# Eight of the 32 pieces of a transposed key cache are prepared during the attention instead of during and right after the input projection

## The reference, cut to what matters

```
h = rms_norm(x, g_pre_mix);  z = h @ w_in           # 2560 columns: q, k, v, a, gate
kc = concatenate([cache_win_k, k], axis=1)          # sample group: cached keys, then new ones
for window, dil in ((128, 1), (512, 4), (2048, 16)):
    idx = wb + t - dil * arange(129)
    s = einsum("bthd,btjhd->bthj", q, kc[:, idx]) * 64 ** -0.5
    o, lse = softmax(s) @ vc[:, idx], log of the denominator
attn = mixture of the three by their denominators
u = a * sigmoid(gate); c = silu(layer_norm(causal_dwconv(u, width 31)))
x = x + rms_norm(concat(rms_norm(attn), rms_norm(c)) @ w_out)
# then cross-attention into 256 memory rows, and a gated convolutional FFN
```

## Time and profile before

| | |
|---|---|
| median of three runs | 1789.27 us |
| the profiled execution's own time | 1791.59 us |
| its span | 1789.8 us |
| mean granted TensorE clock | 0.98 |
| PE busy | 94% |
| DVE busy | 62% |
| ACT busy | 52% |

### The profile page before, as it was taken

How to read it: one execution, slowest core, us unless ns; L and a number is a source line. 1 busy time by engine, 2 the same in 40 slices (tenths; PEclk the granted TensorE clock), 3 DMA queues, 4 the chain that set the end, 5 groups by cost and what they waited for, 6 DMA issues and landing times.

```text
span 1789.8 us, 29564 instructions
## 1 busy us (share of the span) xinstructions
PE 1689.1 (94%) x11614; PEld 1576.5 (88%) x11614; DVE 1110.3 (62%) x2050; ACT 927.0 (52%) x1680; POOL 2.2 (0%) x12
## 2 busy tenths in 40 slices
PE   7999889946999999999999889999999999999998
PEld 6999888924567999988778889999999999999998
DVE  5489896835775687444567567654576533676533
ACT  7444435653566776555456555444545533545533
POOL 0000000000000000000000000000000000000000
PEclk9999999968999999999999899999999999999999
DMA  9998979669432545543443334444444544444443
GB/s 314 242 247 198 231 178 211 130 202 332 170 114 87 170 147 166 163 131 120 144 131 115 94 114 134 141 130 141 132 141 150 151 132 143 130 141 145 146 135 105
DMA packets 417824, 284.02 MB, mean 159 GB/s; under 512 B 69675, under 2 KB 392353, under 8 KB 415887
## 3 DMA queue, kind: packets, MB, share of 16 engines
q1 hardware_dynamic: 412840, 273.31, 54.1%
q10 hardware_dynamic: 4847, 8.83, 1.5%
HBM read 226.97 MB, written 32.48 MB: 145 GB/s over the span
## 4 chain that ended last, share of the span: by engine, by line
PE 76%; DVE 6%; SPq 6%; ACT 5%; DMA 4%; issue 3%; DVEq 0%; ACTq 0%
PE bank L1341 71%; PE bank L1338 4%; DMA PLANES<-HALVES 2%; SPq L473 2%; SPq L528 1%; ACT whi L702 1%; SPq L518 1%; SPq L519 1%; DMA raw<-in_w_in_dram 1%; ACT WORDS L825 1%; DVE C L1931 1%; DVE cv L1931 1%; DVE wlo L1944 1%; DMA raw<-in_w_mk_dram 0%; DMA cached_t<-keys_turned 0%
## 5 line engine op out<-in xcount | busy, mean ns | idle before, releaser
L1944 DVE TENSOR_TENSOR wlo<-raw,whi 128x1024 fp32r<-128x1024 f32 (+1 forms) x312 | 374.3, 1201 | 274.3 <-ACT whi L702 274.0
L1341 PE MATMUL bank<-op_hi,whi 128*128 128x352 f32 x1632 | 539.3, 330 | 4.7 <-DVE wlo L1944 2.4
L1341 PE MATMUL bank<-op_hi,wlo 128*128 128x352 f32 x1632 | 525.8, 322 | 0.0
L1341 PE MATMUL bank<-op_lo,whi 128*128 128x352 f32 x1632 | 524.6, 321 | 0.0
L702 ACT ACTIVATE whi<-raw 128x1024 fp32r<-128x1024 f32 (+1 forms) x312 | 325.1, 1043 | 330.0 <-DMA raw<-in_w_up_dram 92.3
L1341 PEld LDWEIGHTS bank<-op_hi,whi 128*128 128x128 f32 x1632 | 307.4, 188 | 14.3 <-issue 10.5
L1341 PEld LDWEIGHTS bank<-op_lo,whi 128*128 128x128 f32 x1632 | 308.4, 189 | 0.6
L1341 PEld LDWEIGHTS bank<-op_hi,wlo 128*128 128x128 f32 x1632 | 307.4, 188 | 0.0
L1341 PE MATMUL bank<-fhi,whi 128*128 128x352 f32 x528 | 171.1, 324 | 0.0
L1341 PE MATMUL bank<-fhi,wlo 128*128 128x352 f32 x528 | 170.8, 323 | 0.0
L1341 PE MATMUL bank<-h1hi,whi 128*128 128x352 f32 x480 | 160.8, 335 | 3.3 <-DVE wlo L1944 3.3
(11 more groups left out here) (284 smaller groups left out, 2229.7 us busy)
## 6 DMA issues: line engine op xcount, KB each, us to landing
raw<-in_w_up_dram SPq DMA_DIRECT2D x132, 512.0 KB, 3.8
raw<-in_w_down_dram SPq DMA_DIRECT2D x48, 512.0 KB, 4.1
PLANES<-HALVES SPq DMA_DIRECT2D x128, 112.0 KB, 3.7
keys_turned<-WORDS SPq DMA_DIRECT2D x32, 448.0 KB, 3.2
cached_t<-keys_turned SPq DMA_DIRECT2D x8, 1792.0 KB, 8.9
raw<-in_w_out_dram SPq DMA_DIRECT2D x24, 512.0 KB, 4.2
raw<-in_w_xq_dram SPq DMA_DIRECT2D x24, 512.0 KB, 4.1
raw<-in_w_xo_dram SPq DMA_DIRECT2D x24, 512.0 KB, 4.2
```

The costliest lines, as they stand in the source:

```text
L1341: return pe.matmul(out, lhsT, rhs, start=first, stop=last, skip_group_check=shared)
L1944: dve.tensor_tensor(wlo[v % SLOTS][:, 0:nk, :], raw[v % SLOTS][:, 0:nk, :], whi[v % SLOTS][:, 0:nk, :].bitcast(F32), ALU.subtract).then_in ...
```

## The change

Pieces 24 to 31 (sequences 6 and 7) are called LATE. The other 24 are spread over the projection, one to a call place at most, and end before its end. The late ones get their own buffers for halves, planes and words in the first three weight slots, which stand empty until the output projection, and a semaphore name of their own for the joins. SP calls the stream for two of them behind each of windows 3 to 7. ACT joins them at slots r = 10, 16, 18, 23, 25, 30, 32, 39 of the first group, ahead of whatever else that slot holds. The three weight loads of the output projection move from before the V outputs to behind window 7 and the last piece. Two of the three places for windows are swapped, so that window 1 no longer waits for the convolution and window 2 does; three small tiles (STD) move out of the way.

```diff
...
@@ -209,13 +209,15 @@
     stage_f = mn("stage_f", 146656, [P, 3, P])
 
 
-    PLACES = (47104, 119808, 160064)
+    PLACES = (47104, 160064, 119808)
     cached = [mn(f"cached{i}", o, [P, KTILES, AW]) for i, o in enumerate(PLACES)]
     cached_t = [mn(f"cached_t{i}", o, [P, AT, KEYS]) for i, o in enumerate(PLACES)]
     HALVES = [mn(f"HALVES{i}", 160064 + 3584 * i, [P, 2, KEYS], U16) for i in range(2)]
     PLANES = [mn(f"PLANES{i}", 160064 + 7168 + 3584 * i, [P, 2, KEYS], U16) for i in range(2)]
     WORDS = [place(f"WORDS{i}", TAB + 3584 * i, [P, KEYS]) for i in range(2)]
-    WORDS += [place("WORDS2", RING, [P, KEYS]), place("WORDS3", RING + 5504, [P, KEYS])]
+    HALVES += [place(f"HALVES{2 + i}", RING + 3584 * i, [P, 2, KEYS], U16) for i in range(2)]
+    PLANES += [place(f"PLANES{2 + i}", RING + 3584 * (2 + i), [P, 2, KEYS], U16) for i in range(2)]
+    WORDS += [place(f"WORDS{2 + i}", RING + 3584 * (4 + i), [P, KEYS]) for i in range(2)]
     ATT = mn("ATT", 20480, [P, AT, NTOK])
     Pp = [mn("Pp0", 0, [P, 2, SEQ]), mn("Pp1", 8192, [P, 2, SEQ]), place("Pp2", RING + 8192 * (SLOTS - 1), [P, 2, SEQ])]
     PT = mn("PT", 38912, [P, 2, SEQ])
@@ -240,7 +242,7 @@
     XT = [mn("XT0", 20480, [P, NT, CW]), mn("XT1", 31744, [P, NT, CW]), mn("XT2", 0, [P, NT, CW])]
     xtok = [mn(f"xtok{i}", o, [P, D]) for i, o in enumerate((11264, 15360, 43008, 160064, 164160, 168256))]
     Yb = [mn(f"Y{i}", o, [P, NT, CW]) for i, o in enumerate((50176, 129024, 140288))]
-    STD = [place(f"STD{i}", RING + 8192 * i + 4096, [P, CW]) for i in range(CH)]
+    STD = [place("STD0", RING + 21504, [P, CW]), place("STD1", RING + 22912, [P, CW]), mn("STD2", 37376, [P, CW])]
     SQ = [mn(f"SQ{i}", 129024 + 1408 * i, [P, CW]) for i in range(4)]
     CSUM = [mn(f"CSUM{i}", o, [P, CW]) for i, o in enumerate((125440, 126848, 122624))]
     SQA = [mn(f"SQA{i}", 134656 + 1408 * i, [P, CW]) for i in range(4)]
@@ -369,15 +371,17 @@
         return n, n % len(cached)
 
     PIECES = AT * BD
-    LATE = PIECES - 4
-    PIECES_AT = {u: 1 for u in (*range(NT, 3 * NT, 2), 9, 13, 15, 19, 23, *range(3 * NT, XFIRST))}
-    PIECES_AT.update({24: 2, 28: 2, 32: 2, XFIRST: 2, XFIRST + 1: 2})
+    LATE = PIECES - 8
+    PIECES_AT = {u: 1 for u in (*range(NT, 3 * NT, 2), 11, 15, 19, 23, *range(3 * NT, XFIRST), XFIRST)}
 
     def pieces_until(u):
         return sum(n for v, n in PIECES_AT.items() if v < u)
 
-    def words_of(p):
-        return WORDS[p % 2 + (2 if p >= LATE else 0)]
+    def place_of(p):
+        return p % 2 + (2 if p >= LATE else 0)
+
+    def joined_by(p):
+        return "joined_late" if p >= LATE else "joined"
 
     def batch_slot(r):
 
@@ -512,7 +516,7 @@
                 sp.wait_ge(*at(f"planes{p % 2}", (p - 2, 1, 1)))
             if k == 0:
                 sp.wait_ge(*at(f"gathered{b % 2}", b))
-            t, name = HALVES[p % 2], f"turned{p % 2}"
+            t, name = HALVES[place_of(p)], f"turned{p % 2}"
             cols = slice(2 * P * k, 2 * P * (k + 1))
             near = A["cache_win_k"][0, b].rearrange("s h d -> s (h d)").bitcast(U16)[WB - NEAR:WB, cols]
             sp.dma_start_transpose(t[:, :, OLD:KEYS], near).then_inc(*mark(name, (p, "near"), 16))
@@ -522,24 +526,24 @@
 
             sp.wait_ge(*at(f"turned{p % 2}", (p, "old")))
             if p >= 2:
-                sp.wait_ge(*at("joined", (p - 2, 1)))
+                sp.wait_ge(*at(joined_by(p - 2), (p - 2, 1)))
             for e in range(2):
                 for h in range(2):
-                    sp.dma_start(PLANES[p % 2][DH * e:DH * e + DH, h, :], HALVES[p % 2][h:P:2, e, :]).then_inc(*mark(f"planes{p % 2}", (p, e, h), 16))
+                    sp.dma_start(PLANES[place_of(p)][DH * e:DH * e + DH, h, :], HALVES[place_of(p)][h:P:2, e, :]).then_inc(*mark(f"planes{p % 2}", (p, e, h), 16))
 
         def keep_keys(p):
 
             b, k = divmod(p, AT)
-            sp.wait_ge(*at("joined", (p, 1)))
-            sp.dma_start(A["keys_turned"][b, :, k, :], words_of(p)[:, :]).then_inc(*mark(f"kept{p % 2}", p, 16))
-
-        def key_stream(p):
-
-            if p < PIECES:
+            sp.wait_ge(*at(joined_by(p), (p, 1)))
+            sp.dma_start(A["keys_turned"][b, :, k, :], WORDS[place_of(p)][:, :]).then_inc(*mark(f"kept{p % 2}", p, 16))
+
+        def key_stream(p, first, end):
+
+            if first <= p < end:
                 turn_keys(p)
-            if 0 <= p - 1 < PIECES:
+            if first <= p - 1 < end:
                 part_keys(p - 1)
-            if 0 <= p - 2 < PIECES:
+            if first <= p - 2 < end:
                 keep_keys(p - 2)
 
         load(ident[:, :], A["identity"], "ident")
@@ -556,7 +560,7 @@
             if SLOTS <= u < SLOTS + BD:
                 gather_old(u - SLOTS)
             for _ in range(PIECES_AT.get(u, 0)):
-                key_stream(p)
+                key_stream(p, 0, LATE)
                 p += 1
             if u == SLOTS + 1:
                 load(stage_p[0:KW * CT, 1, :], A["conv_w"].rearrange("a t (k p) -> (a t k) p", p=P), "states", "cw")
@@ -568,27 +572,18 @@
                 for i in range(2):
                     load(stage_u[:, i, :], A["state_conv"].rearrange("a b t c -> (a b t) c")[i * 120:(i + 1) * 120, :], "states", ("u", i))
 
-        while p < LATE + 2:
-            key_stream(p)
-            p += 1
+        for p in range(p, LATE + 2):
+            key_stream(p, 0, LATE)
         for i in range(2):
             sp.wait_ge(*at(f"kept{i}", LATE - 2 + i))
         load(wt[:, :], A["prompt_bias"], "tables", "p")
         load(ws[:, :], A["sample_bias"], "tables", "s")
-        key_stream(LATE + 2)
+        window(1)
         sp.wait_ge(*at("unit", LAST_IN))
         window(0)
-        for p in range(LATE + 3, PIECES + 2):
-            key_stream(p)
         sp.wait_ge(*at("csq_used", 2 * CH - 1))
         sp.wait_ge(*at("cn", (CONV_ORDER[CH - 1], CT - 1)))
-        window(1)
-        sp.wait_ge(*at("joined", (PIECES - 1, 1)))
         window(2)
-        for u in range(XFIRST, XFIRST + SLOTS - 1):
-            for i in range(2):
-                sp.wait_ge(*at(f"kept{i}", PIECES - 2 + i))
-            weight(u)
         sp.wait_ge(*at("ztok", ("v", AT - 1, 2)))
         for t in range(TT):
             sp.dma_start(O["win_v_p"][0, 0, t * P:(t + 1) * P].rearrange("s h d -> s (h d)"), V[:, t, :]).then_inc(*mark("v_out", t, 16))
@@ -605,6 +600,14 @@
             else:
                 sp.wait_ge(*at("spv", b))
             window(n)
+            if n < 8:
+                for p in range(LATE + 2 * (n - 3), LATE + 2 * (n - 2)):
+                    key_stream(p, LATE, PIECES)
+            if n == 7:
+                for u in range(XFIRST, XFIRST + SLOTS - 1):
+                    for i in range(2):
+                        sp.wait_ge(*at(f"kept{i}", PIECES - 2 + i))
+                    weight(u)
         for e in range(2):
             sp.wait_ge(*at("ptr", (LAST_P2, parts_of(STEPS[LAST_P2][0]) - 1, e)))
         weight(XFIRST + SLOTS - 1)
@@ -818,11 +822,9 @@
             act.wait_ge(*at(f"planes{p % 2}", (p, 1, 1)))
             if p >= 2:
                 act.wait_ge(*at(f"kept{p % 2}", p - 2))
-            if p in (LATE, LATE + 1):
-                act.wait_ge(*at("unit", LAST_IN - 3 + p % 2))
-            words = words_of(p)[:, :].bitcast(U16).rearrange("p (n h) -> p h n", h=2)
+            words = WORDS[place_of(p)][:, :].bitcast(U16).rearrange("p (n h) -> p h n", h=2)
             for h in range(2):
-                act.activation(words[:, h, :], PLANES[p % 2][:, h, :], ACT.Copy).then_inc(*mark("joined", (p, h)))
+                act.activation(words[:, h, :], PLANES[place_of(p)][:, h, :], ACT.Copy).then_inc(*mark(joined_by(p), (p, h)))
 
         def join_to(n, joined):
 
@@ -895,11 +897,14 @@
                     act.dma_start(O["win_k_p"][0, 0, t * P:(t + 1) * P].rearrange("s h d -> s (h d)"), KS[:, t, :]).then_inc(*mark("ks_out", t, 16))
                 act.dma_start(O["win_k_s"][0].rearrange("b t h d -> (b t) (h d)"), KS[0:NS, TT, :]).then_inc(*mark("ks_out", TT, 16))
 
-        for p in range(joined, PIECES):
-            join_keys(p)
+        assert joined == LATE
+
+        LATE_AT = {10: 0, 16: 1, 18: 2, 23: 3, 25: 4, 30: 5, 32: 6, 39: 7}
 
         def sample(g, r):
 
+            if g == 0 and r in LATE_AT:
+                join_keys(LATE + LATE_AT[r])
             if r == GROUP + 2:
                 act.wait_ge(*at("smax", g))
                 act.activation(Ps[:, :], Ps[:, :], ACT.Exp, bias=negm[:, 2:3], accum_out=den[:, 2:3]).then_inc(*mark("sexp", g))
```

(2 more changed lines are left out.)

## The result

The changed kernel takes 1803.81 us, the median of 5 runs (1800.24 to 1806.15), against 1789.27 us before (5 runs by now, the median is the same); the ratio is 1.0073, with an interval of 1.0054 to 1.0093. So it is slower by 0.7%, where I forecast 1787, a gain too small to measure. The time lies inside the range, 1768 to 1805, but on the other side. The profiled execution of after is its fastest run: own time 1800.24 us, span 1798.4, which is 8.6 longer than before; I work with these 8.6 and keep in mind that the medians stand 14.5 apart.

A forecast was written before the change was run, and what follows sets the result against it. From 120 to 421 us the order on SP, with its key stream, was the bound. Of 48 us won, 6.3 outlast the late stream; less four times 1, 2 us gained: 1789.27 - 2.3 rounded, 1787 us, range 1768 to 1805.

The forecast's parts named there:

- window 3: Window load in SP's list behind window 2 and the V outputs: issued at E + 17, 11.3 us for 19 transfers.
- E: Time at which PE ends the last projection unit: from 360.6 to 336 us, bounds 332 and 350.
- the late stream: Pieces 24 to 31 during attention: first copies landed E + 33 to 34, pieces 25 to 30 take 52 us more.
- the clock: PE's granted clock: 6 us won in the projection; 0.5 to 0.8 in the late stretch, costing 1 us.
- rival D: Projection: DVE paces it, E only to 348, late stream as forecast; 10 us slower, 1799; chance 0.08.
- Step 0: First attention step: its exponentials start at E + 7.1 = 343 instead of 391.5 us, 48 us gained so far.
- upper bound: Pieces 25 to 30 by DMA work: 6 x 7.3 + 3 x 4.7 = 58 us.
- lower bound: Pieces 25 to 30 by chain: 6 x 7.5 = 45 us, and 2 for a wait on ssc.
- Rival C: Late stream: full DMA queues pace it, 11 us a piece; 12 us slower, 1801; chance 0.16.
- Rival B: Late stream is cheaper: 1776, at the far end 1748 with only 18 us of joins paid; chance 0.28.
- step 11: Attention step behind piece 30's join: exponentials start at E + 90 = 426 instead of 432.30 us.
- Behind it: After step 11: join 31, window 8, full DMA queues and the clock cost 1 us each.

The follow-up runs named there:

- Experiment 4: The changed kernel without loads of the cached values of sequences 1 to 3 (windows 5, 6, 7), sequence 0's values read instead: 1789.91 us, ratio 0.9993.
- experiment 7: The changed kernel with late pieces begun before the attention and spread, V outputs last, windows 4 to 6 ahead of pieces: 1748.30 us, 0.9762 of the kernel before.
- `no_late`: The changed kernel with the late stream (pieces 24 to 31) left out whole: 1738.73 us, ratio 0.9701 to the kernel before.
- experiment 2: Two separate moves in the changed kernel: V outputs behind the last window, 1795.64 us; three weights behind window 9 instead of 7, 1797.39 us.
- `spread2`: The kernel of experiment 7: the changed kernel with late pieces begun early and spread, V outputs last, windows 4 to 6 moved ahead: 1748.30 us.
- `no_v_windows`: The kernel of Experiment 4: the changed kernel without loading windows 5, 6 and 7: 1789.91 us, ratio 0.9993 to the kernel before.

## Why the prediction was wrong

The mechanism was in the main the one forecast: the projection gives back its waits, window 3 comes late, ACT stops at slot 10 until the first late copies are there, and each further piece is a wait of some us. Two terms were set too low, E by 5.5 us and the late stream by 5.2, and what stands behind them by 3.4; together they turned a gain of 2 us into a loss.

- *E*, forecast 336, was 341.5: 5.5 us. Of 22.0 us of waits I left 3.5; PE stayed idle for 7.2. Of the clock, now 0.98, I counted 6; what the waits leave of the 19.1 us gained is 4.2. This is the first step that failed: "E = 360.6 - 22 - 6 + 3.5 = 336". Of the waits left, 5.8 us are for ACT's copies, and the longest, 3.5, stands behind a late weight and a join at 200 us; only 1.4 are for DVE, so rival D's reason was not shown. Why the clock gave 4.2 and not 6 stays open. Step 0 stood at E + 6.9 (forecast 7.1).
- *Window 3*, forecast E + 17, came at E + 19.6: the 19 output transfers ahead of it took 14.2 us (346.90 to 361.07) instead of 11.3. The first late copies landed at E + 34.7 (forecast 33 to 34), so little of this was passed on. ACT waited 21.75 us (forecast 21).
- *The late stream* is the second step that failed, and here the mechanism was incomplete: "I take 52, near the middle, for every SP wait leaves some DMA idle." It was 57.1, near my upper bound of 58. The lower bound's 7.5 a piece was right to 0.2 us where no window stood between. But I had put windows only into the bound by DMA work; a values window stands in the chain, with its own issue (2.7 us) and the slower turns behind it, 3.5, 4.1 and 5.1 us for the three. 6 x 7.4 + 12.7 = 57.1. At window 5 (392.90) the 4.1 are 1.2 until the window is issued, past the landing at 394.51 that the turn waits for, 1.9 for the slower issue of the turns, and 1.0 for the copies, which land 3.3 us behind their last issue instead of 2.3. Of window 6's 5.1, 1.2 are SP's wait for the scores of sequence 3, for which I had 2. Experiment 4 shows it: two windows fewer, 7.7 us earlier. The near agreement with the upper bound, 58, is luck: that bound was for DMA engines busy all the time, and they were busy 0.85 of it. Rival C had the sign and half of the mechanism. Window data ahead of the stream and SP's own issues are what it named; full DMA queues as the pace are not borne out, as experiment 7 shows with fuller DMA engines and one wait of 4.4 us.
- *Rival B's* far end, 1748, is the time of experiment 7 (1748.30), with another order than this change has. That it agrees so closely is luck as well: E was 5 us later than it assumed, and 11 us stayed against `no_late` where it counted 18.
- With step 11 some 3.4 behind the last landing (forecast 4) it came at 436.7 instead of 426: 5.5 from E, 5.2 from the stream.
- *Behind it* I had 4 us for join 31, window 8, full queues and the clock; it was 7.4 up to step 31. The three weights ahead of window 8, which I gave a transfer of 2 us, cost up to 6 (experiment 2; the wait for window 8 that went with them was 3.7).
- 2.3 gained - 5.5 - 5.2 - 3.4 + 3 that came back behind the attention = 9 lost, which is the profiled 8.6. The medians differ by 5.9 us more, because the profiled execution of after was 3.6 under its median and that of before 2.3 above.

The 261 GB/s for a turn that the Trainium skill gives ("DMA: Bandwidth & Descriptors", section on latency and other measured facts) stood for rival B's lower end, a chain of 7.5 us a piece; the trace has 7.3 to 7.5 where no window stands between, and more elsewhere. Of the clock: it was 0.58 in the late stretch, the range forecast, and 0.89 in `spread2`, where PE waits little; PE was busy 29.8 and 49.7 of the 62 us. That is in line with the Trainium skill, "TensorE: Matmul & The Clock Gate", section on HAM oscillation, but the runs don't price it apart from the waits.

## What to carry to other kernels

Work moved out of a crowded stage has to be begun there, or its first result is late by the whole length of its chain: moving the joins alone gave 0.4%, moving the beginning of the stream, its place among the windows and the joins together gave 3.1%. Of an in-order DMA list, sum what stands between two links of a chain, large transfers included. A window in front of a turn cost 3.5 to 5.1 us where the join stood ready and waiting; with the joins further off, windows in front of turns and a DMA share of 0.96 cost one wait of 4.4 us. And where two large terms of opposite sign nearly cancel (48 gained, 46 spent), the sign of their difference is worth no more than the bounds of each.

## What the runs showed of the hardware

A DMA transpose pair that takes 2.5 us to issue in after with no window before it (387.11, 406.01) takes 4.2 to 4.5 right behind a 1792 KB window. In the median the two transposes of a pair land 4.8 and 4.4 us behind their issue where windows stand between, and 3.5 and 3.2 in `no_v_windows` where none does. In the fullest stretch of `spread2` one such pair took 7.9 us to issue (404.62 to 412.58). Two moves in the order of issues, at two ends of the one chain, gave 0.48% and 0.35% alone and 0.76% together, each to 0.2 to 0.3%.
